# Gated-delta inverse of a hybrid decoder step: the last z tile, the samples' pairs, a weight split and six state loads take other places

## The chip, the cores and the metric

One core of a Trainium2 chip runs the whole program. The metric is device time in microseconds (us), lower is better. Times are of single executions; the one that was profiled has a span (from the first to the last recorded instruction) and, a little longer, a time of its own.

## What is computed

One inference step of a four-layer decoder trunk, in float32, for 256 prompt tokens and 8 sequences of 4 sample tokens (288 columns in all). The layers' token mixers are gated DeltaNet, latent attention, mLSTM and gated DeltaNet again; each stands between two SwiGLU halves. The change is in the gated DeltaNet mixer, so in layers 0 and 3:

```python
proj = x @ w_in
qkv_pre, z, b, a = jnp.split(proj, [GDN_QKV, GDN_QKV + GDN_Z, GDN_QKV + GDN_Z + GDN_HEADS], axis=-1)
...
a_mat = jnp.eye(L, dtype=jnp.float32) + jnp.einsum('nbhid,nbhjd->nbhij', kb, kc) * decay_strict
rhs = jnp.concatenate([vc * bc[..., None], kb * jnp.exp(gc)[..., None]], axis=-1)
sol = lax.linalg.triangular_solve(a_mat, rhs, left_side=True, lower=True, unit_diagonal=True)
...
o = _rmsnorm(o, norm_w) * jax.nn.silu(z.astype(f32).reshape(B, T, GDN_HEADS, GDN_DV))
y = o.reshape(B, T, GDN_Z).astype(x.dtype) @ w_out
```

L is 64 for the prompt (4 chunks, 8 heads) and 4 for the samples. `S0` is the old state, 8 heads x 8 sequences x 128 x 128, 4 MB for one layer.

## The kernel before, in words

Every engine has its own hand-written list of instructions, and the lists meet only at semaphores (`once(engine, name, value)` waits until a counter has reached a value). So the order of work on an engine is the order of the calls in its function: `pe_gdn` (TensorE), `dve_gdn` (VectorE), `act_gdn` (ScalarE), `pool_gdn` (GpSimd) and `sp_gdn` (the DMA queue of SyncE).

A float32 product of weights and activations is made of three float32r products: weights come as units of 1 MB (`sp_unit`), ScalarE rounds one (`act_split`, L355), VectorE takes the remainder (`dve_split`, L372), and TensorE multiplies hi*hi, hi*lo and lo*hi. The last four of the eight output tiles of z are made late, by `z_tile` (L1292 to L1294, 24 matmuls each), between the parts of the inverse.

The triangular matrices are inverted by doubling, in six levels, for two groups g of four heads:

- `inverse_first` is level 0 (L1393, L1394).
- `inverse_z(l)` (L1404) makes Z = B*X for both groups, 32 instructions of 64x64; VectorE masks the result out of PSUM into R (`masked_z`, L1963).
- `inverse_x(l)` (L1418 and L1421) makes the new X and its transpose from R, 64 instructions; ScalarE copies X out (`x_copy`, L1645), VectorE the transpose (`xt_copy`, L1969). Then the next `inverse_z` can start.

Between these calls stands work that doesn't depend on them: `sample_pairs` (L1365 to L1381, the products within the samples' chunks), `sample_small` (L1435, the samples' own inverse), `turned` (L1354, L1357, transposes of k and v) and `sample_old` (L1447, the samples against the old states of one group). A float32 instruction is recorded as two passes of TensorE, so one `inverse_z` is 64 passes, one `inverse_x` 128, `sample_pairs` 65, `sample_old` 128; a pass has a weight load and a matmul.

`state_in` (L1104) loads the old state of one head, 512 KB in pieces of 512 bytes. `sp_gdn` issues heads 2 and 3 early; then the conv states go out; then heads 4, 5, 6, 7, 0 and 1 follow, each behind a wait that says that the place for it is free, or holds it back until a step of the inverse is done. `sample_old(1)` needs heads 4 to 7, `sample_old(0)` heads 0 to 3.

The lines of the table of signals that matter: `g_x_done`, `g_xt_done` and `g_z_done` count one for each group and level (g_z_done from level 1), so g_z_done 4 is the end of z at level 2, g_xt_done 6 the end of x at level 2.

Of the kernel before, what the change touches and what calls it, by code (L numbers as in the profile page):

```python
# [216 lines left out]
def trunk(nc, a, subs):  # L217
# [29 lines left out]
    def once(eng, name, v):  # L247

        eng.wait_ge(sem(name), v + before(name))

    with ctx:
# [799 lines left out]
        def sp_gdn(sp, n):  # L1051
            gi, u0 = subs[n][2], ubase[n]
            sp.dma_start(crow[:], a["state_gdn_conv"][gi].rearrange("b j c -> (b j) c")).then_inc(sem("g_conv_in"), 16)
            for u in range(u0, u0 + NRAW):
                sp_unit(sp, u)
            once(sp, "unit_used", u0)
            sp.dma_start(gtab[:], a["c_gdn"]).then_inc(sem("g_tab_in"), 16)
            sp.dma_start(gsm[:, 0:1], a["gdn_dt_bias"][gi].rearrange("(h o) -> h o", o=1)).then_inc(sem("g_tab_in"), 16)
            sp.dma_start(gsm[:, 1:2], a["gdn_a_log"][gi].rearrange("(h o) -> h o", o=1)).then_inc(sem("g_tab_in"), 16)
            for u in range(u0 + NRAW, u0 + 17 + 2):  # L1060
                sp_unit(sp, u)
                if u == u0 + 10:
                    state_in(sp, gi, (2, 3))
            once(sp, "g_trow_ready", 2)
            by_quarter = lambda v: v.rearrange("r (k q c) -> r k q c", q=4, c=P)
            for q in range(4):
                sp.dma_start(by_quarter(a["gdn_conv_p"][gi, 0])[:, :, q, :], trow[NS * q:NS * q + 3]).then_inc(sem("g_conv_out"), 16)
                sp.dma_start(by_quarter(a["gdn_conv_s"][gi].rearrange("b j c -> (b j) c"))[:, :, q, :],
                             trow[NS * q + 3:NS * q + 27]).then_inc(sem("g_conv_out"), 16)
            sp.wait_ge(unit_used, u0 + 17)  # L1070
            state_in(sp, gi, (4,))
            once(sp, "g_x_done", 3)
            state_in(sp, gi, (5,))
            once(sp, "g_xt_done", 4)
            state_in(sp, gi, (6,))
            once(sp, "g_z_done", 4)
            state_in(sp, gi, (7,))
            once(sp, "g_d", 2)
            once(sp, "g_s1", 1)
            once(sp, "g_t", 1)  # L1080
            state_in(sp, gi, (0,))
            once(sp, "g_t", 2)
            state_in(sp, gi, (1,))
            once(sp, "g_s5", 2)
            for u in range(u0 + 19, u0 + 21):
                sp_unit(sp, u)
            once(sp, "g_conv_out", 128)
            for g in (1, 0):
                for hh in range(4):
                    h = 4 * g + hh  # L1090
                    once(sp, ("g_s_new", "g_s_odd")[hh % 2], 4 * (1 - g) + 3 + hh // 2)
                    sp.dma_start(a["gdn_S_s"][gi, :, h].rearrange("b d e -> d b e"), S0[h]).then_inc(sem(f"g_s_out{g}"), 16)
            once(sp, "g_s", 8)
            sp.dma_start(a["gdn_S_p"][gi, 0].rearrange("h d e -> d h e"), S[:]).then_inc(sem("g_sp_out"), 16)
            once(sp, "g_s_out0", 64)
            once(sp, "g_s_out1", 64)
            once(sp, "g_sp_out", 16)
# [3 lines left out]
        def state_in(sp, gi, heads):  # L1101

            for h in heads:
                sp.dma_start(S0[h], a["state_gdn_S"][gi, :, h].rearrange("b d e -> d b e")).then_inc(sem(f"g_s_in{h // 4}"), 16)  # L1104
# [61 lines left out]
        def pe_gdn(pe, n):  # L1166
            gi, u0 = subs[n][2], ubase[n]
# [18 lines left out]
            inverse_first(pe, n, 0)  # L1186
            inverse_first(pe, n, 1)
            inverse_z(pe, 1)
            z_tile(pe, n, 7)
            inverse_x(pe, 1)  # L1190
            sample_pairs(pe)
            inverse_z(pe, 2)
            sample_small(pe, 0)
            inverse_x(pe, 2)
            turned(pe, 0)
            sample_small(pe, 1)
            inverse_z(pe, 3)
            turned(pe, 1)
            inverse_x(pe, 3)
            turned(pe, 2)  # L1200
# [195 lines left out]
        def inverse_z(pe, l):  # L1396

            if l == 1:
                once(pe, "g_trow_ready", 2)
            for g in range(2):  # L1400
                once(pe, "g_x", 2 + 2 * (l - 1) + g + 1)
                for q in range(8):
                    for e in range(2):
                        last = pe.matmul(psum[halves(1 - e), ZBANK[g], q * CH:(q + 1) * CH], B[g][halves(e), q, :],  # L1404
                                         X[g][halves(e), q, :], start=True, stop=True)
                last.then_inc(sem("g_z_done"), 1)
# [20 lines left out]
        def sample_small(pe, k):  # L1427

            once(pe, ("g_s_xt", "g_s_x", "g_s_r")[k], 1)
            for g in range(2):  # L1430
                for hh in range(4):
                    c = P * 2 + 64 * k + g * NS
                    lhsT = (XTs, Bs, Rs)[k]
                    rhs = (gt("sid")[quarter(hh), :], Xs[quarter(hh), g, :], XTs[quarter(hh), g, :])[k]
                    last = pe.matmul(psum[quarter(hh), 0, c:c + NS], lhsT[quarter(hh), g, :], rhs, start=True, stop=True)  # L1435
            last.then_inc(sem(f"g_s{2 + k}"), 1)
# [136 lines left out]
        def act_gdn(act, n):  # L1573
# [106 lines left out]
            for g in range(2):  # L1680
                last = act.activation(M2s[:, g].rearrange("q a i -> q (a i)"), psum[:, 0, 64 * g:64 * g + 64], ACT.Exp,
                                      bias=BIAS[:, 16 + g:17 + g])
            last.then_inc(sem("g_dts"), 1)
            once(act, "g_s2", 1)
            act.activation(Xs[:].rearrange("q g i -> q (g i)"), psum[:, 0, 256:320], ACT.Copy).then_inc(sem("g_s_x"), 1)
            x_copy(2, 0)
            x_copy(2, 1)
            act.preload_act_table_set("silu_and_others")
            z_silu(0)
            z_silu(1)  # L1690
# [147 lines left out]
        def dve_gdn(dve, n):  # L1838
# [157 lines left out]
            for e in range(2):  # L1996
# [5 lines left out]
            first_low(1)  # L2002
            z_evacuated(6)
            xt_copy(0)
            dve_split(dve, u0 + 17)
            masked_z(1)
            z_evacuated(7)
            xt_copy(1)
            once(dve, "g_s1", 1)
            once(dve, "g_dts", 1)  # L2010
            m2s = M2s[:].rearrange("q g a i -> q (g a i)")
            step(dve.tensor_tensor(m2s, psum[:, 0, P:2 * P], m2s, ALU.mult))
            step(dve.tensor_tensor(Bs[:], gt("sid")[:, None, :].to_broadcast([P, 2, NS]), M2s[:, :, 1, :], ALU.subtract))
            dve.tensor_tensor(XTs[:], Bs[:], gt("sfirst")[:, None, :].to_broadcast([P, 2, NS]), ALU.mult).then_inc(sem("g_s_xt"), 1)
            masked_z(2)
            once(dve, "g_s1", 2)
            once(dve, "g_ce", 1)
            dve.tensor_tensor(KDs, two(psum[:, 1, 0:256]), sc(2), ALU.mult)
            dve.tensor_tensor(RHS, two(psum[:, 1, 256:512]), sc(0), ALU.mult).then_inc(sem("g_s_kv"), 1)
            xt_copy(2)  # L2020
            once(dve, "g_s3", 1)
            dve.tensor_tensor(Rs[:], psum[:, 0, 320:384].rearrange("q (g i) -> q g i", g=2),
                              gt("slevel")[:, None, :].to_broadcast([P, 2, NS]), ALU.mult).then_inc(sem("g_s_r"), 1)
            once(dve, "g_conv_out", 128)
            k_scaled(0)
            masked_z(3)
            xt_copy(3)
            k_scaled(2)
            masked_z(4)
            xt_copy(4)  # L2030
            k_scaled(4)
            masked_z(5)
# [1689 lines left out]
```

## Time and profile before

| what | value |
|---|---|
| time, median of 3 runs | 2592.34 us (2587.88 to 2593.7) |
| the profiled execution's own time | 2595.06 us |
| its span | 2593.3 us |
| TensorE busy | 2565.2 us (99%), 21903 passes |
| VectorE / ScalarE / GpSimd busy | 60% / 45% / 12% |
| mean granted TensorE clock | 0.995 of full speed |

TensorE is busy nearly all the time, and the chain that ended last is 96% TensorE. Instruction gaps named "issue" are times in which an engine stood still and no semaphore of another engine explains it.

### The profile page before, as it was taken

The numbers are of one execution on the slowest core, as the hardware profiler recorded it, in microseconds if no ns is written. First come the engines' busy times: TensorE is split into PE (matmuls) and PEld (weight loads), VectorE is DVE, ScalarE is ACT, GpSimd is POOL, SyncE is SP. The second block draws the span as 40 slices with busy tenths as digits, with TensorE's granted clock in tenths as the row PEclk, the third lists the DMA queues.
The fourth block names the chain that finished last, engine by engine and source line by source line (L and its number), as shares of the span: only waits on it lengthen the run. The fifth ranks groups of instructions, "written<-read, shape, count | busy, mean of one in ns | idle before, by whom it ended". The sixth has DMA issues, their size and how long they took to land.

```text
span 2593.3 us, 51715 instructions
## 1 busy us (share of the span) xinstructions
PE 2565.2 (99%) x21903; PEld 2452.5 (95%) x21903; DVE 1557.0 (60%) x1938; ACT 1178.8 (45%) x1600; POOL 307.6 (12%) x319
## 2 busy tenths in 40 slices
PE   9999999999999999999999999999999999999999
PEld 8999988999999986799999999799999999979999
DVE  5546966755655545575465554575566549757654
ACT  5334745544444444453353443353344337545443
POOL 1001015100100155010010000010020001052000
PEclk9999999999999999999999999999999999999999
DMA  6445625454554546444455465365454455235543
GB/s 219 162 137 170 179 73 156 152 167 140 175 169 143 192 135 186 147 153 162 151 173 164 144 193 158 108 193 163 140 184 163 135 179 174 93 110 175 167 140 113
DMA packets 417309, 404.24 MB, mean 156 GB/s; under 512 B 14940, under 2 KB 413400, under 8 KB 416824
## 3 DMA queue, kind: packets, MB, share of 16 engines
q1 hardware_dynamic: 412888, 397.38, 48.6%
q0 software_dynamic: 4096, 4.20, 0.6%
q8 instruction: 136, 2.23, 0.4%
q14 instruction: 45, 0.37, 0.0%
q10 hardware_dynamic: 144, 0.07, 0.0%
HBM read 385.22 MB, written 16.39 MB: 155 GB/s over the span
## 4 chain that ended last, share of the span: by engine, by line
PE 96%; DVE 2%; ACT 1%; issue 1%; DMA 0%; SPq 0%; DVEq 0%; ACTq 0%
PE psum L392 24%; PE psum L394 24%; PE psum L393 24%; PE psum L716 2%; PE psum L712 2%; PE psum L713 2%; PE psum L3112 1%; PE psum L1404 1%; PE psum L3125 1%; PE psum L1447 1%; PE psum L494 1%; PE psum L3150 1%; PE psum L1501 0%; PE psum L2302 0%; PE psum L2303 0%
## 5 line engine op out<-in xcount | busy, mean ns | idle before, releaser
L372 DVE TENSOR_TENSOR w_lo<-raw,w_hi 128x2048 fp32r<-128x2048 f32 (+3 forms) x361 | 740.0, 2050 | 503.8 <-ACT w_hi L355 503.7
L392 PE MATMUL psum<-xn_hi,w_hi 128*128 128x288 f32 x3232 | 960.7, 297 | 0.5 <-DVE w_lo L372 0.2
L393 PE MATMUL psum<-xn_lo,w_hi 128*128 128x288 f32 x3232 | 953.4, 295 | 0.0
L394 PE MATMUL psum<-xn_hi,w_lo 128*128 128x288 f32 x3232 | 950.4, 294 | 0.0
L355 ACT ACTIVATE w_hi<-raw 128x2048 fp32r<-128x2048 f32 (+2 forms) x349 | 596.9, 1710 | 776.7 <-PE psum L394 760.3
L392 PEld LDWEIGHTS psum<-xn_hi,w_hi 128*128 128x128 f32 x3232 | 605.6, 187 | 5.9 <-issue 3.8
L394 PEld LDWEIGHTS psum<-xn_hi,w_lo 128*128 128x128 f32 x3232 | 608.6, 188 | 0.0
L393 PEld LDWEIGHTS psum<-xn_lo,w_hi 128*128 128x128 f32 x3232 | 606.7, 188 | 0.7
L393 PE MATMUL psum<-h_lo,w_hi 128*128 128x288 f32 x1408 | 415.5, 295 | 0.0
L394 PE MATMUL psum<-h_hi,w_lo 128*128 128x288 f32 x1408 | 414.9, 295 | 0.0
L392 PE MATMUL psum<-h_hi,w_hi 128*128 128x288 f32 x1408 | 414.8, 295 | 0.0
L392 PEld LDWEIGHTS psum<-h_hi,w_hi 128*128 128x128 f32 x1408 | 264.7, 188 | 0.4
L393 PEld LDWEIGHTS psum<-h_lo,w_hi 128*128 128x128 f32 x1408 | 264.6, 188 | 0.4
L394 PEld LDWEIGHTS psum<-h_hi,w_lo 128*128 128x128 f32 x1408 | 264.7, 188 | 0.0
L450 POOL TENSOR_TENSOR fbuf<-sq 128x576 f32<-128x576 f32 x21 | 42.9, 2042 | 1592.8 <-ACT sq L742 1381.6
L888 DVE TENSOR_TENSOR sg<-psum,rr 128x576 f32<-128x576 f32 x81 | 61.3, 757 | 158.9 <-PE psum L394 157.7
L851 ACT ACTIVATE h_hi<-fbuf 128x576 f32 (+1 forms) x88 | 60.3, 685 | 207.7 <-DVE fbuf L915 207.7
L918 DVE TENSOR_TENSOR h_lo<-fbuf,h_hi 128x576 f32 (+1 forms) x88 | 66.7, 758 | 81.6 <-ACT h_hi L851 81.6
L454 POOL TENSOR_TENSOR fbuf<-fbuf,sq 128x576 f32<-128x576 f32 x30 | 64.9, 2163 | 142.4 <-ACT sq L742 139.8
L1874 DVE SCALAR_TENSOR_TENSOR g_cacc<-g_cbuf,vec,g_cacc 128x312 f32<-128x312 f32 x144 | 73.7, 553 | 1.7
L915 DVE TENSOR_TENSOR fbuf<-sg,fbuf 128x576 f32<-128x576 f32 x88 | 66.2, 753 | 5.3 <-DVE fbuf L908 4.8
L727 DVE TENSOR_SCALAR y<-psum,vec 128x288 f32<-128x288 f32 x96 | 45.7, 510 | 26.7 <-ACT sq L742 20.8
(646 smaller groups left out, 3173.4 us busy)
## 6 DMA issues: line engine op xcount, KB each, us to landing
raw<-w_ffn_up SPq DMA_DIRECT2D x175, 1024.0 KB, 5.1
raw<-w_ffn_down SPq DMA_DIRECT2D x64, 768.0 KB, 4.4
raw<-w_ffn_down SPq DMA_DIRECT2D x64, 640.0 KB, 4.0
raw<-gdn_w_in SPq DMA_DIRECT2D x32, 1024.0 KB, 5.7
raw<-mlstm_w_in SPq DMA_DIRECT2D x12, 1024.0 KB, 5.4
raw<-gdn_w_out SPq DMA_DIRECT2D x8, 1024.0 KB, 5.8
raw<-cache_mla_latent SPq DMA_DIRECT2D x64, 128.0 KB, 2.5
a_split<-cache_mla_latent SPq DMA_DIRECT2D x64, 128.0 KB, 2.3
```

The lines of the kernel that those rows point to most:

```text
L355: act.activation(spread(w_hi[slot(u, i)], u), packed(raw[u % NRAW], u), ACT.Copy).then_inc(hi_ready, 1)
L372: dve.tensor_tensor(spread(w_lo[slot(u, i)], u), packed(raw[u % NRAW], u), spread(w_hi[slot(u, i)], u).bitcast(F32), ALU.subtract).then_in ...
L392: pe.matmul(out, wh[:, k, c], hi(k), start=st, stop=False)
L393: pe.matmul(out, wh[:, k, c], lo(k), start=False, stop=False)
L394: last = pe.matmul(out, wl[:, k, c], hi(k), start=False, stop=sp_)
L454: pool.tensor_tensor(sq_part, sq_part, sq[:, 2 * i:2 * i + 2, :], ALU.add).then_inc(sum_step, 1)
L712: pe.matmul(out, hi[:, k, c], xn_hi[:, k, :], start=k == 0, stop=False)
L851: act.activation(dst, fbuf[:, j % 2], ACT.Copy).then_inc(hhi_done, 1)
L888: dve.tensor_tensor(sg[:, j % 2], psum[:, s:s + 2, 0:T], r2, ALU.mult).then_inc(gate_ready, 1)
L915: dve.tensor_tensor(fbuf[:, j % 2], sg[:, j % 2], fbuf[:, j % 2], ALU.mult).then_inc(h_done, 1)
L918: dve.tensor_tensor(h_lo[:, sl, :], fbuf[:, j % 2], h_hi[:, sl, :].bitcast(F32), ALU.subtract).then_inc(hlo_done, 1)
L1874: last = stt(out=dst, in0=cbuf[:, i % 2, k, j:j + CW - 3], scalar=vec[:, r:r + 1], in1=dst, op0=ALU.mult, op1=ALU.add)
```

## The change

Four edits, all in the gated DeltaNet mixer; no arithmetic is added or removed.

1. TensorE: `inverse_x(1)` now stands right behind `inverse_z(1)`, and `z_tile(7)` behind `inverse_x(1)` rather than before it; `sample_pairs` stands between `inverse_z(2)` and `inverse_x(2)` rather than before both; `turned(0)` and `sample_small(1)` are parted by `inverse_z(3)`.
2. VectorE: the split of the first unit of w_out (`dve_split(u0 + 17)`) moves from before level 1's mask to behind level 4's; the samples' small steps, `k_scaled(0)` and the copies are put in the order in which TensorE now makes their operands.
3. ScalarE: level 2's two copies of X come before the samples' copy `Xs`.
4. SyncE: the six late state loads wait for other counters: one for the z tile and then one for each half level.

```diff
@@ sp_gdn
             sp.wait_ge(unit_used, u0 + 17)
             state_in(sp, gi, (4,))
-            once(sp, "g_x_done", 3)
+            once(sp, "g_z_done", 4)
             state_in(sp, gi, (5,))
-            once(sp, "g_xt_done", 4)
+            once(sp, "g_xt_done", 6)
             state_in(sp, gi, (6,))
-            once(sp, "g_z_done", 4)
+            once(sp, "g_z_done", 6)
             state_in(sp, gi, (7,))
             once(sp, "g_d", 2)
             once(sp, "g_s1", 1)
             once(sp, "g_t", 1)
+            once(sp, "g_xt_done", 8)
             state_in(sp, gi, (0,))
             once(sp, "g_t", 2)
+            once(sp, "g_z_done", 8)
             state_in(sp, gi, (1,))
@@ pe_gdn
             inverse_z(pe, 1)
+            inverse_x(pe, 1)
             z_tile(pe, n, 7)
-            inverse_x(pe, 1)
+            inverse_z(pe, 2)
             sample_pairs(pe)
-            inverse_z(pe, 2)
+            inverse_x(pe, 2)
             sample_small(pe, 0)
-            inverse_x(pe, 2)
             turned(pe, 0)
+            inverse_z(pe, 3)
             sample_small(pe, 1)
-            inverse_z(pe, 3)
             turned(pe, 1)
             inverse_x(pe, 3)
@@ act_gdn
             last.then_inc(sem("g_dts"), 1)
+            x_copy(2, 0)
+            x_copy(2, 1)
             once(act, "g_s2", 1)
             act.activation(Xs[:].rearrange("q g i -> q (g i)"), psum[:, 0, 256:320], ACT.Copy).then_inc(sem("g_s_x"), 1)
-            x_copy(2, 0)
-            x_copy(2, 1)
@@ dve_gdn
             xt_copy(0)
-            dve_split(dve, u0 + 17)
             masked_z(1)
+            xt_copy(1)
             z_evacuated(7)
-            xt_copy(1)
+            masked_z(2)
             once(dve, "g_s1", 1)
...
-            masked_z(2)
             once(dve, "g_s1", 2)
...
             xt_copy(2)
+            once(dve, "g_conv_out", 128)
+            k_scaled(0)
+            masked_z(3)
             once(dve, "g_s3", 1)
...
-            once(dve, "g_conv_out", 128)
-            k_scaled(0)
-            masked_z(3)
             xt_copy(3)
             k_scaled(2)
             masked_z(4)
+            dve_split(dve, u0 + 17)
             xt_copy(4)
```

TensorE's instructions around level 2's z, before (line numbers of the kernel before; L1365 to L1381 are the samples' pairs, L1435 the samples' inverse):

```order
L1365 MATMUL psum<-g_smaskr,g_identr 128x128
L1370 MATMUL psum<-y,g_tab 32x64 x8
L1375 MATMUL psum<-g_qkv 32x64 x8
L1381 MATMUL psum<-base,g_qkv 32x128 x16
L1404 MATMUL psum<-g_x_87,g_b_85 64x64 x16
L1404 MATMUL psum<-g_x_88,g_b_86 64x64 x16
L1435 MATMUL psum<-g_tab,g_xts 32x32 x8
```

And as changed, where every line number is higher by 2:

```order
L1406 MATMUL psum<-g_x_87,g_b_85 64x64 x16
L1406 MATMUL psum<-g_x_88,g_b_86 64x64 x16
L1367 MATMUL psum<-g_smaskr,g_identr 128x128
L1372 MATMUL psum<-y,g_tab 32x64 x8
L1377 MATMUL psum<-g_qkv 32x64 x8
L1383 MATMUL psum<-base,g_qkv 32x128 x16
L1420 MATMUL psum<-fbuf,g_xt_89 64x64
```

The pairs moved from before z to between z and x of the same level. The 24 matmuls of `z_tile(7)`, which stood between z and x of level 1, stand behind that x now.

VectorE's instructions from level 0's copy of the transpose on, before (L372 is the split, L1963 the mask, L1958 takes the z tile, L2012 to L2019 are the samples'):

```order
L1969 COPY g_xt_89<-psum 128x512
L1969 COPY g_xt_90<-psum 128x512
L372 TENSOR_TENSOR w_lo<-raw,w_hi 128x2048
L1963 TENSOR_TENSOR fbuf<-psum,g_tab 128x512 x2
L1958 TENSOR_TENSOR g_z<-psum,rr 128x288
L1969 COPY g_xt_89<-psum 128x512
L1969 COPY g_xt_90<-psum 128x512
L2012 TENSOR_TENSOR g_m2s<-psum,g_m2s 128x128
L2013 TENSOR_TENSOR g_bs<-g_tab,g_m2s 128x64
L2014 TENSOR_TENSOR g_xts<-g_bs,g_tab 128x64
L1963 TENSOR_TENSOR fbuf<-psum,g_tab 128x512 x2
L2018 TENSOR_TENSOR y<-psum,g_ce 128x256
```

And as changed:

```order
L1971 COPY g_xt_89<-psum 128x512
L1971 COPY g_xt_90<-psum 128x512
L1965 TENSOR_TENSOR fbuf<-psum,g_tab 128x512 x2
L1971 COPY g_xt_89<-psum 128x512
L1971 COPY g_xt_90<-psum 128x512
L1960 TENSOR_TENSOR g_z<-psum,rr 128x288
L1965 TENSOR_TENSOR fbuf<-psum,g_tab 128x512 x2
L2014 TENSOR_TENSOR g_m2s<-psum,g_m2s 128x128
L2015 TENSOR_TENSOR g_bs<-g_tab,g_m2s 128x64
L2016 TENSOR_TENSOR g_xts<-g_bs,g_tab 128x64
L2019 TENSOR_TENSOR y<-psum,g_ce 128x256
L2020 TENSOR_TENSOR sq<-psum,g_ce 128x256
```

The split is gone from before the mask of level 1, and level 2's mask stands ahead of the samples' steps; the split follows the mask of level 4.

## Rows read from the trace of the kernel before

**Rows 1.** The page's chain that ended last, by engine.
```profile
PE 96%; DVE 2%; ACT 1%; issue 1%; DMA 0%; SPq 0%; DVEq 0%; ACTq 0%
```
**Rows 2.** The chain in order of time, layer 0's inverse: start us, us, what.
```profile
356.64 0.33 PE psum L1292
...
360.03 0.20 PE psum L1418
...
362.06 0.26 PE psum L1365
...
363.90 1.36 PE psum L1404 x41
365.27 1.78 issue
367.04 0.91 PE psum L1404 x23
367.95 0.26 PE psum L1435 x16
...
369.65 1.00 issue
...
372.31 2.01 PE psum L1404 x64
...
376.92 1.48 issue
...
389.82 0.14 issue
```
**Rows 3.** The same chain, layer 3's inverse.
```profile
2270.07 1.60 PE psum L1404 x49
2271.66 0.96 issue
...
2275.12 1.97 issue
...
2278.78 3.31 PE psum L1404 x64
...
2295.92 0.34 issue
```
**Rows 4.** Engines' busy time in 2278 to 2282 us, with granted clock, DMA share, GB/s.
```profile
2278.00:2282.00 4.00, 4.00 (x84) 3.68 (x82) 2.67 (x5) 2.97 (x4) 0.00 (x0) 0.57 0.45 133
```
**Rows 5.** The page's DMA queues: packets, MB, share; only the instruction queue q8.
```profile
q8 instruction: 136, 2.23, 0.4%
```
**Rows 6.** The DMA queues in 356 to 357 us; only q8.
```profile
q8 instruction: 1, 0.02, 6.6%
```
**Rows 7.** The DMA queues in 364 to 365 us; only the instruction queue.
```profile
q8 instruction: 1, 0.02, 7.6%
```
**Rows 8.** The DMA queues in 364 to 392 us, then in 391 to 392 us; only q8.
```profile
q8 instruction: 8, 0.13, 1.8%
...
q8 instruction: 1, 0.02, 7.1%
```
**Rows 9.** The data queue in 361.5 to 367.1 us, and then in 376.5 to 378.6 us.
```profile
q1 hardware_dynamic: 2980, 1.50, 102.4%
...
q1 hardware_dynamic: 977, 0.49, 80.5%
```
**Rows 10.** State loads as SyncE issues them, by time, layer 0.
```profile
360.06 1.48 SPq L1104 DMA_DIRECT2D g_xn<-state_gdn_S  x2
...
362.14 0.37 SPq L1104 DMA_DIRECT2D g_xn<-state_gdn_S  x1
...
374.94 0.37 SPq L1104 DMA_DIRECT2D y<-state_gdn_S  x1
```
**Rows 11.** VectorE by time around level 1's mask, layer 0.
```profile
355.28 2.28 DVE L372 TENSOR_TENSOR w_lo<-raw,w_hi 128x2048 fp32r<-128x2048 f32 x1
357.48 1.28 DVE L1963 TENSOR_TENSOR fbuf<-psum,g_tab 128x512 f32<-128x512 f32 x2
```

## The prediction

> **What bounds the kernel now.** I read the page first. The chain that ended last is 96% TensorE and 1% "issue" [rows 1]: there is little to win but TensorE's own standstills. So I went to the chain in order of time, in the two stretches that the change touches. There TensorE never waits for VectorE, ScalarE or a load. What it has are gaps named issue: 1.78, 1.00, 1.48 and 0.14 us in layer 0 [rows 2], 0.96, 1.97 and 0.34 us in layer 3 [rows 3], 7.67 us together. Behind the second pair of gaps of layer 3 the clock falls: it is granted at 0.57 of full speed over 4 us [rows 4], that is partly the level of 1.2 GHz, and z at level 3 takes 3.31 us [rows 3] where the same work takes 2.01 us in layer 0 [rows 2]: 1.30 us more. Together 8.97 us, 0.35% of the time. This is all that the change can give back.
>
> **What the gaps are.** Count the passes between them. From the end of the first gap (367.04) to the second (369.65): 23 passes of z, 16 of the samples, and 1.44 us of x, which at 128 passes in 2.03 us (360.03 to 362.06) is 91: 130 in all. From 370.65 to 376.92: the other 37 of x, 4, 16, 64, 4 and nearly all 128 of the next x, about 253. From 378.40 to 389.82: 2, 4, 16, 64, 4, 128, 128, 16 and 21, so 383 [rows 2]. That is one, two and three times 128. The instruction queue q8 moved 136 packets with 2.23 MB, 16.4 KB each [rows 5], which is 128 bytes for each of 128 passes. In 28 us there are 8 such packets, the first in the microsecond at 364, the last in that at 391 [rows 7, 8]: seven intervals of 3.7 to 4.0 us. TensorE's instructions come in blocks of 128 passes, and a block comes no sooner than about 3.8 us after the one before. From 367.04 to 389.95 TensorE went through six blocks in 22.9 us, 3.82 us each: **this stretch runs at the pace of the instruction blocks**, and the gaps are where dense work (x: 63 passes per us) spends a block in less.
>
> The first gap is of another kind. Its block is entered 41 passes into z [rows 2]; the block before it was entered 128 passes earlier, at about 361.7, so it took 5.3 us rather than the 3.6 us from 367.04 to 370.65. In between, heads 4, 5 and 6 are loaded together, issued at 360.06 (two) and 362.14 [rows 10]: 1.50 MB in 5.6 us, with the data queue at 102% of the engines' time [rows 9]. A single load (0.49 MB in 2.1 us, 80%) [rows 9] ran across the third gap.
>
> Here a rule stands against my reading. The Trainium skill, "Runtime: NRT & Kernel Launch", section "Instruction fetch mechanics", says that an engine's instructions are refilled in blocks of 16 KiB by a queue of its own, and the size agrees with 16.4 KB [rows 5]. But it calls the cost of crossing a block mostly hidden, since instructions are dispatched more slowly than blocks come; by that rule these gaps are something else, and spreading loads gives nothing: 2592.3 us. The trace's own count of 128 passes weighs more with me.
>
> **The change, part by part.** I lay out layer 0 from 356.64 on (end of z at level 1) by the rows: x 2.03, z 2.01, z tile 3.39 (356.64 to 360.03), pairs 1.84 (362.06 to 363.90), samples' small step 0.26 us [rows 2]; the transposes of 4 passes take about 0.6 us (372.31 less 371.7). Work between 356.64 and 389.95 is 33.31 less 4.40, 28.91 us, before and after. Only the gaps change. Counting passes from 356.64, block edges lie at 130, 258, 385, 513, 640, 768, 895 and 1023.
>
> - Edge 130, before in the middle of x at level 1, with 24 slow matmuls of the z tile ahead of it. Now x stands first: the edge is reached 2 passes into the z tile, at 358.9. Its packet is in the microsecond at 356 [rows 6]; the block behind the packet at 364 was usable at 367.04, 2 to 3 us later. So it is there at 359.0 to 359.9: a **new gap** of 0.1 to 1.0 us, I take 0.5. In layer 3 z stops 49 passes in, not 41 [rows 2, 3]: edges are 8 passes later, which in the z tile is 1.1 us, so 0 to 0.5, I take 0.2.
> - Edge 258: z tile and z at level 2 stretch this block to 6 us, and the pairs get the edge. No gap: the 1.78 and 0.96 us go.
> - Edge 385, in x at level 2: the block is 24 passes of the pairs and 104 of x, 2.3 us of work against 3.6 to 3.8 us. Up to 1.5 us are missing; but where nothing stalled before, the ask comes up to a microsecond early (the packet at 356 [rows 6] is there as TensorE enters the block before its own, 2 passes into the z tile at 356.9, where otherwise 3.6 us lie between entry and use and only the last 2 to 3 of them behind the packet's start). Head 5's load, now issued at the end of z at level 2, runs across this block, as single loads ran across the second and third gap. Between 0.5 and 2.0 us; I take 1.1 and 0.9 (layer 3) for 1.00 and 1.97 us before.
> - Edge 513: 4.1 us of work, no gap, as before.
> - Edge 640, all of x at level 3: 2.0 us of work. Head 7's load, issued at the end of z at level 3, again meets the block. 1.4 us as before (1.48) in layer 0, 1.1 in layer 3, where half clock had given time for it; bounds 0.8 and 2.0.
> - Edges 895 and 1023: 0.5 and 0.7 us (before 0.14 and 0.34), since the chain of blocks arrives only a little earlier than before.
> - Clock: no gap over 1.5 us, so no fall in layer 3: the 1.30 us go. If it falls again, once, they stay; twice, 1.3 us more.
>
> Layer 0: 0.5 + 1.1 + 1.4 + 0.5 = 3.5 against 4.40 us, so 0.9 less. Layer 3: 0.2 + 0.9 + 1.1 + 0.7 = 2.9 against 3.27 + 1.30, so 1.67 less. Sum 2.6; Worked the other way, as a chain of blocks (edge 385's at 368.3 + 1.1 = 369.4, then five at 3.8 to 4.0 us), the stretch ends at 389.2 and not 389.95: 0.8 less for each layer, 1.6 in all. I take 2.3, between the two.
>
> What costs nothing, and its cover. The split (2.28 us) [rows 11] moves to where VectorE has only the masks behind it: `sample_old(1)` keeps TensorE busy for 128 passes meanwhile, and the product with w_out that needs it is over 50 us away. Without the move, x at level 1 would have to wait: the mask began at 357.48 and took 1.28 us [rows 11], so until 358.8, with x now due at 356.64. Moved, the masks follow z directly: the first is done before 356.64, the second at 357.4, and x needs it only for its second half, at 357.65; 0.3 us of cover, and 0 to 0.4 us lost for each layer if it doesn't hold. ScalarE's order: x copies come earlier, the samples' Xs 0.6 us later, before 2 us of z. State loads: head 7 is now issued at about 373, and a load took 4 to 5 us to land; `sample_old(1)` comes at about 380. Head 1 (before 374.94) [rows 10] at about 379, 10 us before its use. Behind SyncE's waits are only the w_out units, which need the end of the samples' products anyway.
>
> The profiled execution took 2595.06 us: 2592.8 after the change. The median shown is 2.7 us lower, 2592.34, and the forecast is made for it: **2590.0 us**.
>
> **The rivals.**
> - *The burst is the whole cause.* All gaps lie in or next to a state load. If spread loads leave the block's path free, gaps over 0.3 us vanish: 7.67 + 1.30 less about 2 us, so 7 us: 2585.3. For it: the first gap. Against it: the third gap has one load only, and the last (0.14, 0.34 us) none. 0.19.
> - *Not faster but slower: every half level meets its own load.* Head 5's load starts just as the block at edge 385 is asked for, and head 7's the same at edge 640. It decides if a single load delays a block as the three did, 5.3 us rather than 3.6. Then each layer has gaps of 1.0 + 2.8 + 2.5 + 0.7 = 7.0 us, 2.6 us more than layer 0's 4.40, and the clock may fall in both: 2592.3 + 5.2 = 2597.5, and up to 2600. Against it: the single load across the third gap came with a 1.48 us gap, which the work of the block explains alone. 0.07.
> - *Nothing moves.* The gaps aren't blocks (the rule above), or what the new gap in the z tile takes equals what the pairs give: 2592.3. 0.11.
>
> **How the numbers follow.** My forecast has 0.63, the rivals 0.19, 0.07 and 0.11. About 0.2% (5.2 us) is what a measurement of this kernel can tell from no change; runs shown differ by 6 us. Faster by more: the first rival and 0.03 of the forecast, 0.22. Slower by more: 0.07. Between: 0.71. The forecast's own range is 2587 to 2593.5 (bounds of edges 130, 385, 640); with the spread of medians and most of the first rival 2585 to 2595.
>
> **What would show it.** Right: no gap in z or in the pairs at level 2; gaps of 0.5 to 2 us in x at level 2 and at level 3, and a short one early in the z tile or none; q8 still one packet per 3.7 to 4.0 us from there on; no clock below 1.00 at 2278 to 2282; x at level 1 right behind z. Wrong: gaps in x at levels 2 and 3 gone (first rival), or over 2 us each (second); waits of TensorE on L1965, or of L1449 on a state load.

## The result, and the profile after

| | before | after |
|---|---|---|
| median | 2590.7 us (8 runs, 2587.88 to 2593.7) | 2598.65 us (8 runs, 2594.4 to 2600.64) |
| ratio | | 1.0029, 95% interval 1.0018 to 1.0040 |
| profiled execution, its span | 2595.06, 2593.3 us | 2600.4, 2598.7 us |

The change costs 8 us (by the interval 5 to 10), which is more than the 0.2% that can be told from no change. Forecast were 2590.0 us and a range that ends at 2595: wrong, and on the other side. Further runs of before have medians of 2589.8 to 2590.4 us, 2 us under the 2592.34 that was shown ahead. So it is fairer to compare the changes: 2.3 us less was forecast and 8 us more was measured, a miss of about 10 us.

The page of after: the same work on TensorE, the same share of it in the chain. VectorE, ScalarE and GpSimd show no new bound.

```profile
PE 2565.2 (99%) x21903; PEld 2451.8 (94%) x21903; DVE 1559.2 (60%) x1938; ACT 1178.5 (45%) x1600; POOL 307.4 (12%) x319
...
PE 96%; DVE 2%; issue 1%; ACT 1%; DMA 0%; SPq 0%; DVEq 0%; ACTq 0%
```

The chain in order of time (start us, us, what), layer 0's inverse and then layer 3's, answers [rows 2, 3]:

```profile
357.65 0.89 issue
...
367.17 1.56 issue
...
373.00 0.20 PE psum L1420
...
375.02 3.04 issue
...
378.35 1.04 PE psum L1356 x4
...
379.77 2.86 PE psum L1406 x64
...
387.57 0.94 issue
...
391.93 0.14 issue
...
2277.19 1.76 issue
...
2285.90 2.36 issue
...
2288.58 2.69 PE psum L1406 x64
...
2291.27 1.04 PE psum L1356 x4
2292.32 4.01 PE psum L1449 x128
...
2297.17 0.66 issue
...
2301.36 0.33 issue
```

Line numbers are two higher than before: L1420 and L1423 are x, L1406 is z. The gaps stand where the count of passes put them: two passes into the z tile, none in the pairs, then in x at level 2 (367.17, 2277.19), at the end of x at level 3 (375.02; in layer 3, where the count is a few passes further on, at 2285.90, two passes into the samples' step behind it), in x at level 4 (387.57, 2297.17) and in z at level 5. What is wrong is their size. The one at x at level 3 is 3.04 and 2.36 us where [rows 2, 3] have 1.48 and nothing. Behind it the clock falls, now in both layers. The next rows are engines' busy time in 378 to 383 and in 2286 to 2292 us; the clock is the number behind POOL's, 0.66 and 0.80 (partly the level of 1.2 GHz, as in [rows 4]):

```profile
378.00:383.00 5.00, 4.93 (x90) 4.36 (x89) 3.00 (x5) 0.34 (x2) 0.00 (x0) 0.66 0.39 108
2286.00:2292.00 6.00, 3.74 (x82) 3.49 (x81) 2.50 (x5) 2.43 (x4) 0.00 (x0) 0.80 0.31 90
```

That costs more than z alone: four transposes of L1356 take 1.04 us there (0.59 elsewhere), z 2.86 and 2.69 (2.01), the samples' old states in layer 3 4.01 (3.63). So 1.3 us in layer 0 and 1.5 in layer 3. Gaps are 6.57 and 5.22 us. Together 14.6 us, against 8.97 of before: 5.6 more, where I had forecast 2.3 less. (The 8.97 count z alone at the low clock; with the transposes and the samples' steps of that stretch they would be about 9.2.)

**Why the longest gap is long.** The packet of the block that ends it starts late. First SyncE's issue of head 7's load, then the DMA queues in 375 to 375.5 us (packets, MB, share of time):

```profile
372.20 0.37 SPq L1106 DMA_DIRECT2D g_xn<-state_gdn_S  x1
```
```profile
q1 hardware_dynamic: 304, 0.15, 100.6%
q8 instruction: 1, 0.02, 14.5%
```

Head 7's first pieces move at 373.2 us, 1.0 us after the issue, and the bulk of its data from 374.0 to 375.5 us. TensorE enters the block before at 373.0 and is through with it at 375.02. The packet for the next starts at 375.4, when the data is nearly through, and is 4.9 us behind the packet before it (370.5), where 3.7 to 4.0 us are the mean of [rows 7, 8]. The block is then usable at 378.06.

### The profile page after: what moved, and what is told of

Same layout as the page of the kernel before. It is cut to its first block, busy times and chain, and to the rows that moved or that the text cites. A ratio compares the mean times of both kernels' runs of the same rounds, so it can differ in the third digit from the quotient of the medians.

```text
span 2598.7 us, 51719 instructions
## 1 busy us (share of the span) xinstructions
PE 2565.2 (99%) x21903; PEld 2451.8 (94%) x21903; DVE 1559.2 (60%) x1938; ACT 1178.5 (45%) x1600; POOL 307.4 (12%) x319
## 3 DMA queue, kind: packets, MB, share of 16 engines
q8 instruction: 136, 2.23, 0.4%
## 4 chain that ended last, share of the span: by engine, by line
PE 96%; DVE 2%; issue 1%; ACT 1%; DMA 0%; SPq 0%; DVEq 0%; ACTq 0%
PE psum L392 24%; PE psum L393 24%; PE psum L394 24%; PE psum L716 2%; PE psum L712 2%; PE psum L713 2%; PE psum L3114 1%; PE psum L1406 1%; PE psum L3127 1%; PE psum L3152 1%; PE psum L1449 1%; PE psum L494 1%; PE psum L1503 0%; PE psum L2304 0%; PE psum L2305 0%
## 5 line engine op out<-in xcount | busy, mean ns | idle before, releaser
L372 DVE TENSOR_TENSOR w_lo<-raw,w_hi 128x2048 fp32r<-128x2048 f32 (+3 forms) x361 | 741.1, 2053 | 502.2 <-ACT w_hi L355 502.0
```

Of the source, the lines that this page charges most:

```text
L372: dve.tensor_tensor(spread(w_lo[slot(u, i)], u), packed(raw[u % NRAW], u), spread(w_hi[slot(u, i)], u).bitcast(F32), ALU.subtract).then_in ...
```

## The experiments

Each gap below is an "issue" row of the chain. The table has the sums of those over 0.1 us at block edges, "clock" being what z takes over 2.01 us; the text goes through them. The time is a median, the sums are of the one execution that was profiled, which lies up to 3 us from it.

| kernel | time, ratio with interval | gaps + clock, layer 0 / layer 3 |
|---|---|---|
| before | 2590.7 | 4.40 / 3.27 + 1.30 |
| before, once more | 2590.1 | 3.72 + 1.27 / 3.12 + 0.24 |
| after | 2598.65, 1.0029 [1.0018, 1.0040] | 6.57 + 0.85 / 5.22 + 0.68 |
| new order, waits of before | 2594.4, 1.0015 [1.0006, 1.0024] | 3.58 + 1.36 / 2.82 + 1.21 |
| old order, new waits | 2596.64, 1.0027 [1.0018, 1.0036] | 5.07 / 4.09 + 1.50 |
| before, hardly any load | 2589.06, 0.9993 [0.9984, 1.0003] | 2.45 / 1.67 |
| after, hardly any load | 2586.41, 0.9986 [0.9977, 0.9995] | 2.35 / 1.38 |
| after, loads behind blocks | 2588.94, 0.9996 [0.9987, 1.0005] | 3.02 / 2.23 |
| before, loads behind blocks | 2589.7, 1.0000 [0.9991, 1.0009] | 2.65 / 4.19 |
| after, head 7 alone moved | 2593.03, 1.0007 [0.9998, 1.0016] | 5.27 / 2.84 |
| before, head 7 alone late | 2594.99, 1.0019 [1.0010, 1.0028] | 3.91 + 1.12 / 5.54 + 1.38 |
| after, loads behind blocks, z tile in halves | 2589.23, 0.9994 [0.9985, 1.0003] | 1.98 / 2.92 |
| after, split early again | 2597.68, 1.0028 [1.0017, 1.0039] | 4.03 + 1.09 / 3.58 + 0.92 |

### Order and waits apart

The diff has two halves: the order of the work (TensorE's list with that of VectorE and ScalarE) and SyncE's waits ahead of the loads. `e1_order_new_waits_old` is after with this taken back:

```diff
-            once(sp, "g_z_done", 4)
+            once(sp, "g_x_done", 3)
             state_in(sp, gi, (5,))
-            once(sp, "g_xt_done", 6)
+            once(sp, "g_xt_done", 4)
             state_in(sp, gi, (6,))
-            once(sp, "g_z_done", 6)
+            once(sp, "g_z_done", 4)
             state_in(sp, gi, (7,))
...
-            once(sp, "g_xt_done", 8)
             state_in(sp, gi, (0,))
...
-            once(sp, "g_z_done", 8)
             state_in(sp, gi, (1,))
```

> The changed kernel's order on TensorE, VectorE and ScalarE, with the state loads' waits of the kernel before. In the new order two of those waits are met when the z tile ends, so heads 4, 5 and 6 are issued together there and head 7 two microseconds later. Theory L (a state load issued in the two microseconds before TensorE's next instruction block is asked for delays the block by up to the load's own 1.5 us; the order of the work by itself is nearly neutral): one long gap of 3 to 5 us in x at level 2, about 1.5 us in x at level 3, none of 3 us there; time within 3 us of the changed kernel's 2598.7. Rival O (the new order itself costs, the loads don't): 2598.7, gaps as in the changed kernel (1.6 and 3.0 us). Rival W (the new waits alone cost): back to the kernel before, 2590.7.

`e2_order_old_waits_new` is before with the same lines the other way round.

> The kernel before with only the new waits of the state loads. Theory L: the 1.78 us gap in z at level 2 shrinks to about 1, but head 7's load, issued at the end of z at level 3, meets the block that x at level 3 needs: that gap grows from 1.48 to about 3 us, and head 1's makes one of 0.5 to 1 us in x at level 4; 2593 to 2597 us, so 2 to 6 us slower than before. Rival O: 2590.7, no gap of 3 us. Rival W: all of the loss, 2598.7.

Both are slower than before: 2594.4 and 2596.64 us against 2589.84, so +4.6 and +6.8. (The first was expected at 2595.7 at the least.) The waits alone, without the new order, bring most of what the whole change costs. The chain of `e2_order_old_waits_new` in layer 0:

```profile
364.31 0.29 issue
...
367.21 0.73 issue
...
374.21 2.63 issue
...
384.91 1.01 issue
```

The pairs' edge of [rows 2] has shrunk (1.78 to 0.29), for the burst of three loads is gone: that part of the change does what it should. But x at level 3 has 2.63 us for 1.48, and x at level 4 1.01 us where there was nothing. (In layer 3 x at level 3 has no gap; there the clock falls behind one of 2.24 us in x at level 2, which gives the blocks time.) With the new order and the old waits it is x at level 2 that meets the burst, and the clock falls behind it:

```profile
366.94 2.96 issue
...
371.32 3.37 PE psum L1404 x64
```

### Hardly any load traffic

`e3_before_no_load_traffic` and `e4_after_no_load_traffic` load one sequence of eight for heads 0, 1 and 4 to 7 and put zeros in the place of the others, so most of the samples' old state is left out. The issues, their waits and TensorE's work stay; GpSimd's filling and a wait of its own come in.

```diff
             for h in heads:
-                sp.dma_start(S0[h], a["state_gdn_S"][gi, :, h]...)
+                nb = NB if h in (2, 3) else 1
+                sp.dma_start(S0[h][:, 0:nb], a["state_gdn_S"][gi, 0:nb, h]...)
...
             for g in (1, 0):
+                if g == 0:
+                    once(pool, "g_t", 2)
+                for h in (range(4, 8) if g == 1 else range(2)):
+                    pool.memset(S0[h][:, 1:NB], 0.0)
```

> The kernel before, where the six late state loads bring only the first of eight sequences (64 KB rather than 512 KB each) and GpSimd fills the rest with zeros, so the samples' part of the gated DeltaNet mixer works on a mostly empty old state. It takes the loads' traffic away and leaves every wait. Theory L: gaps left are those of the blocks' own pace: about 0 to 0.3 in z at level 2, 1.0 in x at level 2, 1.3 to 1.5 in x at level 3, so 2586 to 2588 us (3 to 4 less than 2590.7). Rival B (loads are the whole cause): no gap over 0.3 us, 2583 us. Rival N (the gaps are not of fetched blocks or traffic): gaps as before, 2590.7.

> The changed kernel with the same cut of the loads' traffic (one sequence of eight loaded, zeros for the rest). Theory L: the long gaps shrink to the blocks' own pace: 0.9 early in the z tile of layer 0, 0.7 to 1.2 in x at level 2, 1.3 to 1.5 in x at level 3, none in x at level 4; 2586 to 2589 us, within 2 us of the kernel before with the same cut. Rival O (the order itself costs): still 6 to 8 us over the kernel before with the same cut.

The gaps don't vanish, they shrink to what the work of the blocks leaves. In before's order:

```profile
366.51 1.25 issue
...
374.03 1.20 issue
```

and in after's:

```profile
358.60 0.73 issue
...
367.95 0.48 issue
...
374.72 1.14 issue
```

The clock doesn't fall in either. Instruction packets of the first start at 361.7, 365.0, 368.9, 372.7, 376.3, 380.0, 383.8 and 387.1 us: 3.63 us apart in the mean. In 356 to 392 us, 4.1% of the engines' time went to data:

```profile
q1 hardware_dynamic: 864, 0.39, 4.1%
...
q8 instruction: 9, 0.15, 1.7%
```

So the pace isn't made by the loads (with all of them, `b2_before_again` below has packets at 362.4, 366.0, 369.4 and 373.1 us, 3.6 us apart). And with the traffic gone, the new order is no worse than the old: 2586.41 against 2589.06 us, gaps of 3.7 against 4.1 us in all. All of the loss hangs on the loads. The time of the first was forecast 1 to 3 us too low: half of its gaps is gone and only 0.8 us of its time, inside the interval. So a sum of gaps isn't yet a time.

### The same loads, each behind a block

If a load hurts only while it is on its way when a block is asked for, the same loads with the same bytes cost nothing a step later. `e5_after_loads_behind_blocks`, from after:

```diff
-            once(sp, "g_z_done", 4)
+            once(sp, "g_s1", 1)
             state_in(sp, gi, (5,))
             once(sp, "g_xt_done", 6)
             state_in(sp, gi, (6,))
-            once(sp, "g_z_done", 6)
-            state_in(sp, gi, (7,))
             once(sp, "g_d", 2)
-            once(sp, "g_s1", 1)
-            once(sp, "g_t", 1)
+            once(sp, "g_t", 2)
+            state_in(sp, gi, (7,))
             once(sp, "g_xt_done", 8)
             state_in(sp, gi, (0,))
-            once(sp, "g_t", 2)
-            once(sp, "g_z_done", 8)
+            once(sp, "g_t", 4)
             state_in(sp, gi, (1,))
```

> The changed kernel with three of the six state loads issued at other points, all as TensorE enters a new instruction block or just after, so that the load runs once that block's successor is on its way and not before it is asked for: head 5 behind the samples' first products rather than the end of z at level 2, head 7 behind the second transposes (turned(1)) rather than the end of z at level 3, head 1 behind turned(3) rather than the end of z at level 4. Theory L: the 3.04 and 2.36 us gaps in x at level 3 shrink to about 1.5, the 0.94 and 0.66 us gaps in x at level 4 to 0.3 or less, no 0.57 clock; 4 to 7 us less than the changed kernel, so 2591 to 2594. Rival O (order and number of loads in the stretch matter, not when exactly one is issued): 2597 to 2599, gap of 3 us stays.

`e6_before_loads_behind_blocks` does it in the order of before: head 4 behind `g_xt_done` 4, head 5 behind `g_z_done` 3, head 6 behind `g_s1` 1 and `g_xt_done` 6, then 7, 0 and 1 as above.

> The kernel before with its order of work and the six state loads issued as blocks are entered: heads 4 (end of x at level 1), 5 (half of z at level 2), 6 (end of x at level 2), 7 (turned(1)), 0 (end of x at level 3), 1 (turned(3)). Theory L: gap in z at level 2 0.3 us or less (1.78 and 0.96 before), about 1.0 in x at level 2, about 1.4 in x at level 3; 2 to 4 us less than the kernel before, so 2586 to 2588. Rival O: like the kernel before with the new waits (2596.6), since the loads are spread over the levels here too.

The first takes back everything: 2588.94 us, 9.7 less than after and 2 less than expected, with three waits moved by a step each. Its chain in layer 0:

```profile
358.47 1.15 issue
...
368.24 0.48 issue
...
375.01 1.39 issue
```

The gap of 3.04 us is 1.39, and x at level 4 has none in this layer (1.14 in layer 3). Head 7's load goes out at 373.08, 0.9 us later than in after, and now the block's packet comes first. The DMA queues in 373.5 to 374 us hold the packet (at 373.53) and no data:

```profile
q8 instruction: 1, 0.02, 14.9%
```

In the order of before the gaps of layer 0 are small too, those of layer 3 are not (1.68, 0.77, 1.14, 0.60), and the time is before's: 2589.7 us, 2 to 4 more than expected.

### One load alone

`e8_after_head7_moved` is after with only head 7's load moved, as above:

```diff
-            once(sp, "g_z_done", 6)
-            state_in(sp, gi, (7,))
             once(sp, "g_d", 2)
             once(sp, "g_s1", 1)
-            once(sp, "g_t", 1)
+            once(sp, "g_t", 2)
+            state_in(sp, gi, (7,))
```

> The changed kernel with one wait different: head 7's load is issued behind turned(1), about 1 us later than the end of z at level 3. Theory L (a load issued just before the next block is asked for delays it by its own length): the gap in x at level 3 falls from 3.04 to about 1.4 us in layer 0 and from 2.36 to 0.7 to 1.2 in layer 3, and the clock doesn't fall behind it; those in x at level 2 (1.56, 1.76) and level 4 (0.94, 0.66) stay; 3 to 5 us less than the changed kernel: 2593.5 to 2596. Rival (the late loads cost by their number in the stretch): 2598 to 2599.

`e9_before_head7_late` is before with head 7's load where after has it:

```diff
-            once(sp, "g_z_done", 4)
+            once(sp, "g_z_done", 6)
             state_in(sp, gi, (7,))
```

> The kernel before with one wait different: head 7's load waits for the end of z at level 3 rather than level 2. Head 0's load, whose own wait is met by then, follows at once, so 1 MB goes out just before the block for x at level 3 is asked for. Theory L: that gap grows from 1.48 to 3 us or more in both layers, the one in x at level 2 shrinks a little (1.00, 1.97 before), the clock may fall; 2 to 5 us more than the kernel before: 2592 to 2595. Rival (order or new waits elsewhere cost): 2590.

The one load gives back 5.6 of the 8 us (2593.03) and, put in alone, costs 4.6 (2594.99). In the first the gap is 1.95 us in layer 0, not the 1.4 that were expected, and 0.98 in layer 3; the clock doesn't fall behind either. In the second the load isn't alone at the edge: heads 7, 0 and 1 go out within 2 us,

```profile
371.89 0.37 SPq L1104 DMA_DIRECT2D g_xn<-state_gdn_S  x1
```

and the x at level 3 that begins behind it has

```profile
374.46 2.30 issue
```

In layer 3 the forecast gap of 3 us at x at level 3 did not come: the clock had fallen behind 1.97 us in x at level 2, x at level 3 has no gap, and x at level 4 has 1.67 us.

Set side by side, the runs give the gap by the issue's distance to the edge (x at level 3, layer 0; "into the block" is the time from TensorE's entry into its last block to the packet for the next):

| kernel | load issued | before the gap | packet behind the last one | packet into the block | gap |
|---|---|---|---|---|---|
| no traffic (after's order) | | | 3.7 us | 0.6 us | 1.14 |
| loads behind blocks, z tile in halves | 372.98 | 1.9 us | 4.0 us | 0.8 us | 1.12 |
| loads behind blocks | 373.08 | 1.9 us | 3.7 us | 0.6 us | 1.39 |
| before, once more | 372.53 | 2.0 us | 3.8 us | 0.6 us | 1.48 |
| before | 374.94 | 2.0 us | 4.0 us | 1.0 us | 1.48 |
| head 7 moved | 372.76 | 1.9 us | 4.6 us | 1.4 us | 1.95 |
| before, head 7 late | 371.89 | 2.6 us | 5.0 us | 1.9 us | 2.30 |
| old order, new waits | 371.64 | 2.6 us | 5.2 us | 2.1 us | 2.63 |
| after | 372.20 | 2.8 us | 4.9 us | 2.4 us | 3.04 |

A load's first pieces move 1.0 us after the issue, the bulk 1.7 to 1.9 us after it, for 1.5 us. TensorE enters its last block 2.0 us before the gap. Where nothing disturbs it, the packet for the next block starts 0.6 us later; in after it is 2.4. In the three kernels with an issue 2.6 to 2.8 us before the gap the first pieces are moving when the packet is due, and it comes 1.3 to 1.8 us late. With an issue 1.9 to 2.0 us before, they come behind that moment and the gap is 1.1 to 1.5 us (before's packet is 0.4 us late behind the data of head 0, which moves until 375.6). One row doesn't fit: with head 7 alone moved the issue is as late, nothing of the load moves from 373.0 to 373.8 us, and the packet, due at 373.3, still starts at 374.08. So the distance decides most of it, over 1.5 us of gap for 0.9 us in the issue from after to loads behind blocks, but not all.

### Are they blocks at all?

`e7_edges_shifted` is before with 32 passes more (the last 32 of the pairs are done twice). If edges lie at every 128 passes, every later gap comes 32 passes earlier in the work.

```diff
-                        last = pe.matmul(psum[quarter(hh), 1, c:c + P], ...)
+                        for _ in range(2):
+                            last = pe.matmul(psum[quarter(hh), 1, c:c + P], ...)
```

> The kernel before with 32 more passes in the samples' pairs (their last 16 instructions are made twice, same results), 0.9 us for each layer. If TensorE's gaps stand at the edges of instruction blocks of 128 passes, each edge behind it falls 32 passes earlier in the work: in layer 0 the gap in z at level 2 comes after 9 passes (41 before), the one in x at level 2 after 56 (88 before), the one in x at level 3 after 94 (126 before); in layer 3 after 17 of z (49 before), 64 of x (96 before). If the gaps stand at the loads or at a place of the code (rival), they stay after 41, 88 and 126 passes.

```profile
363.41 0.43 PE psum L1405 x9
363.84 1.78 issue
...
371.75 1.19 PE psum L1405 x35
372.94 0.67 issue
```

The gap that stood after 41 passes of z at level 2 stands after 9, to the pass, with its 1.78 us. Those in x at level 2 and 3 stand after 56 and 94 passes, as expected, with 0.92 and 0.31 us; the edge between them now falls into z at level 3, after 35 passes, and has 0.67 us. In layer 3 the expectation forgot that layer 0's 32 extra passes carry over: the shift there is 64, and the gaps agree with that (49 passes into the doubled loop; 11 into z at level 3, 50 into z at level 4). The time, 2596.86 us, is that of a single execution, 7 us above before's median for 1.8 us of added work; it isn't explained here.

### Before, once more

Before's own profile was taken of an execution above its median. `b2_before_again` is the unchanged kernel.

> The kernel before, profiled once more, to see how much its gaps differ from one execution to the next. The first profile was of a 2595.06 us execution, and the median of the runs is 2589.8. Theory L: the same gaps within 0.5 us in layer 0 (1.78, 1.00, 1.48), since work and loads keep step there; in layer 3 the clock may not fall, 1.3 us less. If the gaps come at other passes or are gone, their count of 128 is chance.

```profile
363.39 1.51 issue
...
367.52 0.73 issue
...
374.51 1.48 issue
...
377.11 3.28 PE psum L1404 x64
```

Gaps differ by some tenths and the clock falls in layer 0 instead of layer 3, behind a gap of 1.48 us. With this profile the loss can be followed through the program. The samples' update of the state, first and last start, of this run and then of after:

```profile
L1501 PE MATMUL psum<-g_ym,y x64: 587/640/692, 409.1 to 2331.4; 32*128 32x512 f32 x64
```
```profile
L1503 PE MATMUL psum<-g_ym,y x64: 587/640/692, 412.7 to 2341.7; 32*128 32x512 f32 x64
```

After is 3.6 us behind when layer 0's inverse is done and 10.3 us when layer 3's is. The same view of the transposes ahead of each inverse puts 3.2 us of it into layer 0's stretch and 3.9 into layer 3's. The other 3.2 lie where the change touches nothing, and where the granted clock differs from one execution to the next (1600 to 1650 us: 0.97 in after, 1.00 here). This is why times differ from the sums of the table by 1 to 4 us, and why small steps need many runs.

### The z tile's gap, and the split's place

`e10_z_tile_in_halves` is the kernel with loads behind blocks, and with 12 matmuls of the z tile put ahead of x at level 1, so that the edge's block has more slow work in it.

```diff
             inverse_z(pe, 1)
+            z_tile(pe, n, 7, 0)
             inverse_x(pe, 1)
-            z_tile(pe, n, 7)
+            z_tile(pe, n, 7, 1)
             inverse_z(pe, 2)
```

> The kernel e5 (changed order, loads behind the blocks) with the last z tile in two halves of 12 matmuls, one before and one behind x at level 1. Theory L: the block that ends at edge 130 now holds 1.7 us of slow work and x, 3.6 us in all, so the gap in the z tile (1.15 us in layer 0) goes, the others stay (about 0.5 in x at level 2, 1.4 and 0.7 in x at level 3, 1.1 in x at level 4 of layer 3); 0.5 to 2 us less than e5: 2587 to 2588.5. Rival: no gain, 2589.

The gap in the z tile (1.15 us) is gone; x at level 2 has 0.86 us for 0.48. In layer 3 the gaps are 0.7 us more than without. 2589.23 against 2588.94 us: no difference, a gap taken away early comes back in part later.

`e11_after_split_early` is after with the weight split back ahead of the second mask.

```diff
             xt_copy(0)
+            dve_split(dve, u0 + 17)
             masked_z(1)
...
             masked_z(4)
-            dve_split(dve, u0 + 17)
```

> The changed kernel with the split of the w_out unit back in its old place, before level 1's mask. The forecast gave this edit no cost because of its cover. Here x at level 1 stands right behind z and must wait for the mask, which the 2.28 us split holds up: a wait of TensorE on VectorE of about 2 us at the start of x at level 1 in both layers, and the gap of 0.89 us in the z tile of layer 0 is taken up by it; 2.5 to 4.5 us more than the changed kernel: 2601 to 2603. If the split's place doesn't matter: 2598.7.

x at level 1 does wait for the mask, 1.7 us at most and 3.3 us in the two layers together (the view of waits: who waits, for whom, sum, count, longest):

```profile
PE psum L1420 <- DVE fbuf L1965: 3.3, 2, 1.7
```

Yet the time is 2597.68 us, no more than after's, where 2601 to 2603 were expected. Its gaps are 7.6 us rather than 11.8, with the waits 10.9: much of what TensorE waits for the mask it doesn't stand at the edges. x at level 3 in layer 0 has 0.41 us in place of 3.04, but z ahead of it ran at the lower clock (3.10 us) and gave its block time as well, so the single gap can't be put down to the wait.

## Why the prediction was wrong

**The mechanism held.** Blocks of 128 passes: shown by the shift of exactly 32 passes. A pace of its own of about 3.7 us for a block: shown with hardly any traffic, where the gaps at the dense x stay. All edges of after stood where the count put them, 130 in the z tile, none in the pairs, 385, 640, 895 and 1023.

**The term that was mis-sized is the price of one load at an edge.** The forecast wrote for edge 640 "Head 7's load, issued at the end of z at level 3, again meets the block", and took 1.4 and 1.1 us, since the single load of [rows 9] had met the third gap and it was 1.48 us. The load was issued at 372.20 and the gap was 3.04 and 2.36 us; with the load 0.9 us later it is 1.39, without its traffic 1.14. The load of [rows 9] had been issued at 374.94 [rows 10], 2 us before its gap: the packet started at 375.91 and the load's first pieces at 375.97, so its data came behind the packet. I had read "during the gap" as "ahead of it", and took the cheap case as the price of both. That is 2.9 us of 8.2, the distance from the forecast's 6.4 us of gaps and clock (3.5 and 2.9) to the 14.6 measured. The fall of the clock behind these gaps, for which the forecast had nothing, is another 2.8.

**By the other terms** (forecast, measured, us, both layers): edge 130: 0.7, 1.0 (0.89 and 0.11). Edge 385: 2.0, 3.3 (1.56 and 1.76). Edge 640: 2.5, 5.4. Edges 895 and 1023: 1.2, 2.1; head 1's new wait, which I had costed at nothing, lets its load go at 382.73, a block before x at level 4. With that load moved too, layer 0's 0.94 us are gone, but layer 3 then has 1.14 there, so this term isn't settled. Clock: 0 against 2.8.

**The clock.** "No gap over 1.5 us, so no fall" failed on its condition: the gaps were longer. But the rule itself isn't one either. The clock fell behind 3.04, 2.96, 2.82 and 2.36 us, behind 1.97 in before itself, and behind 1.48 in before's second profile; it did not behind 1.78 [rows 2], 1.95 (head 7 moved) and 2.63 (`e2_order_old_waits_new`). The length of the gap alone doesn't settle it. It also falls where no edit reaches: with head 7 moved the granted clock was 0.53 from 1075 to 1086 us, which alone puts that profiled execution (2596.01 us) above its median.

**The rivals.** The one on the other side, "every half level meets its own load", is what came, in its direction, in gaps of 7.0 us a layer (6.57 and 5.22 measured) and in the clock falling in both layers. Its terms did not come one by one: it had 2.8 us for x at level 2 (1.56 and 1.76 measured) and 2.5 for x at level 3 (3.04 and 2.36). That its 2597.5 us lies so near to 2598.65 is in part luck, since it adds 5.2 us to a median that was 2 us too high, and 8 were measured. I gave it 0.07. Its condition was stated rightly (does a single load delay a block as three did?), and the evidence against it was the one gap just named. Of three loads together the trace already had a block that took 5.3 us; nothing excluded that one at the wrong moment does nearly the same, and the packets of after, 4.9 us apart, say that it does. "The burst is the whole cause" fell: with next to no traffic gaps of 0.5 to 1.25 us stay at the dense x. "Nothing moves" fell with it.

**What cost nothing.** The state loads' lateness: no row of TensorE waits for one. ScalarE's order: no row either. The split's cover was needed as I said (without it x waits 1.7 us), but its price wasn't seen in the time: the gaps of that kernel are smaller by more than its waits.

The rule weighed ahead (the Trainium skill, "Runtime: NRT & Kernel Launch", "Instruction fetch mechanics": the cost of crossing a block is mostly hidden) doesn't hold for this stretch: 128 passes of x take 2.03 us against 3.7 for a block, and 3.7 us of gaps stay in the two layers together with next to no traffic.

**What stays open.** Why a block is late: whether its packet waits for a DMA engine, behind the load's pieces there, or whether the request itself is late, was not tried, and the late packet of `e8_after_head7_moved`, with none of the load moving, says that waiting behind its pieces can't be all. The third of the loss that this kernel leaves (2.6 us of its median) isn't placed: edges 385 and 895 still have 1.29 and 1.01 us in layer 0, but its two stretches lose 8.1 us in all, no more than before's two profiles (8.97 and 8.35). And no version that loads the whole state is shown to be faster than before: the three with loads behind blocks lie within 0.1% of it.

## What to carry to other kernels

Where short instructions follow densely, count passes from gap to gap: if the count is a multiple of one number and a packet of the instruction queue goes with each, the stretch has a pace of its own, and work moved, waits removed or loads spread within it come back at the next edge. Put loads there behind the packet of a dense block (moving three took 9.7 us off here, but only back to the time of before), and time them from the packet's start and the load's first data, not from the gap. A transfer that overlaps a gap is not the same as one that was under way when the gap's block was asked for: look at which came first before you take its price from such a row.

## What the runs showed of the hardware that I had not expected

- One load of 512 KB, issued 2.6 to 2.8 us before an edge, goes with a block's packet that comes 4.9 to 5.2 us behind the last one for 3.7, though the packet is only 16.4 KB.
- The pace of blocks hardly depends on traffic otherwise: packets 3.63 us apart with 4.1% of the engines' time in use, 3.6 us with all loads in before's second profile.
- A fall of the clock costs 1.3 to 1.5 us here, since it lasts over z and the transposes beside it, and in one kernel it comes now in layer 0 (z 3.28 us), now in layer 3 (3.31).
- Two waits for another engine of 3.3 us together, ahead of such stretches, cost no measurable time (2597.68 for 2598.65 us).
